# Experts ranked by rows and paired 64/64 or 96/32 in four column strips, raw rows gathered once for two passes

## The reference

```python
def grouped_moe(xn, router_w, router_bias, w1, w3, w2):      # xn = rms_norm(h, gain), 256 x 1024
    aff = sigmoid(xt @ router_w)                              # 256 x 16
    sel = aff + router_bias
    # the best group of 4 experts by the sum of its two largest sel; in it the two largest
    w = aff of the two chosen / their sum;  gate = w spread over 16 experts
    h = silu(xt @ w1[e]) * (xt @ w3[e])                       # w1, w3: 16 x 1024 x 512
    y = sum over e of (h * gate[e]) @ w2[e]                   # w2: 16 x 512 x 1024
```

## Time and profile before

| | |
|---|---|
| median of 3 runs | 566.75 us |
| the profiled execution | 565.24 us |
| its span (first to last instruction) | 563.5 us |
| mean granted TensorE clock | 0.973 |
| PE busy | 531.6 us (94%) |
| PE weight loads | 349.5 us (62%) |
| DVE, ACT busy | 208.5 us (37%), 172.6 us (31%) |
| moved by DMA | 144.67 MB |

### The profile page before, as it was taken

The page is one execution under the profiler, slowest core; times in us unless marked ns, Lnnn a source line. Parts: engine busy times, 40 slices in busy tenths (PEclk is TensorE's granted clock), DMA queues, the critical chain, the costliest instruction groups (busy, mean ns, idle before and its releaser), DMA issues.

```text
span 563.5 us, 7211 instructions
## 1 busy us (share of the span) xinstructions
PE 531.6 (94%) x2808; PEld 349.5 (62%) x2809; DVE 208.5 (37%) x314; ACT 172.6 (31%) x259; POOL 13.8 (2%) x29
## 2 busy tenths in 40 slices
PE   4999999699899999998988999999999999999994
PEld 3898998488578888887854444544444544454442
DVE  4858675657335285555381111111111111111113
ACT  3645557656714243542311111111111111111113
POOL 7100000000000000000000000000000000000000
PEclk9999999989959999999969999999999999999998
DMA  9985445213310653969870997999929979999971
GB/s 314 347 295 183 164 169 186 98 54 135 117 47 2 233 214 109 381 224 374 305 287 12 379 387 289 389 387 386 387 70 380 387 281 391 387 387 386 387 284 75
DMA packets 70950, 144.67 MB, mean 257 GB/s; under 512 B 1873, under 2 KB 3937, under 8 KB 70930
## 3 DMA queue, kind: packets, MB, share of 16 engines
q1 hardware_dynamic: 70274, 142.62, 69.9%
q0 software_dynamic: 656, 1.78, 0.9%
HBM read 143.35 MB, written 1.05 MB: 256 GB/s over the span
## 4 chain that ended last, share of the span: by engine, by line
PE 88%; DVE 5%; ACT 4%; issue 1%; DMA 1%; DVEq 0%; SPq 0%; ACTq 0%
PE bank L1448 34%; PE bank L1207 25%; PE bank L1194 9%; PE bank L1435 7%; PE bank L1511 3%; DVE ring_lo L752 1%; PE bank L1331 1%; PE bank L1330 1%; PE bank L1492 1%; DMA work<-in_norm_mix_gain 1%; PE bank L1165 1%; PE bank L1410 1%; PE bank L1475 1%; ACT diff L607 1%; PE bank L1305 1%
## 5 line engine op out<-in xcount | busy, mean ns | idle before, releaser
L1448 PE MATMUL bank<-ring,work 128*64 128x512 f32 x864 | 191.4, 595 | 2.3 <-issue 2.0
L1448 PEld LDWEIGHTS bank<-ring,work 128*64 128x64 f32 x864 | 61.7, 137 | 113.0 <-issue 111.8
L752 DVE TENSOR_TENSOR ring_lo<-ring,w_hi 128x2048 fp32r<-128x2048 f32 x38 | 86.2, 2286 | 25.7 <-ACT w_hi L550 25.7
L550 ACT ACTIVATE w_hi<-ring 128x2048 fp32r<-128x2048 f32 x37 | 70.3, 1910 | 69.2 <-PE bank L1207 42.5
L1435 PEld LDWEIGHTS bank<-work,xn 128*128 128x128 f32 x320 | 40.4, 199 | 9.2 <-issue 7.3
L1435 PE MATMUL bank<-work,xn 128*128 128x128 f32 x320 | 42.9, 286 | 0.0
L1142 DVE TENSOR_TENSOR ye_lo<-bank,ye_hi 128x512 fp32r<-128x512 f32 x18 | 12.4, 692 | 77.5 <-ACT ye_hi L717 77.5
L1207 PE MATMUL bank<-w_hi,x_hi 128*128 128x512 f32 x144 | 39.3, 395 | 0.4 <-DVE work L788 0.4
L1207 PE MATMUL bank<-w_hi,x_lo 128*128 128x512 f32 x144 | 38.6, 390 | 0.0
L1207 PE MATMUL bank<-ring_lo,x_hi 128*128 128x512 f32 x144 | 38.6, 390 | 0.0
L707 ACT ACTIVATE work<-bank 128x512 f32<-128x512 f32 x9 | 5.4, 597 | 93.9 <-PE bank L1448 93.9
(11 more groups left out here) (241 smaller groups left out, 535.1 us busy)
## 6 DMA issues: line engine op xcount, KB each, us to landing
ring<-in_moe_w SPq DMA_DIRECT2D x64, 1024.0 KB, 13.9
ring<-in_moe_w SPq DMA_DIRECT2D x16, 2048.0 KB, 15.8
ring<-in_w_in SPq DMA_DIRECT2D x13, 2048.0 KB, 8.3
ring<-in_w_out SPq DMA_DIRECT2D x2, 2048.0 KB, 11.3
ring<-in_w_in SPq DMA_DIRECT2D x2, 1024.0 KB, 6.7
ring<-in_w_up_b SPq DMA_DIRECT2D x1, 2048.0 KB, 7.5
ring<-in_w_up_c SPq DMA_DIRECT2D x1, 2048.0 KB, 7.5
ring<-in_w_up_a SPq DMA_DIRECT2D x1, 2048.0 KB, 7.5
```

Of the source, the lines that this page charges most:

```text
L550: act.activation(hi(q), raw(q), ACT.Copy).then_inc(w_hi_ready, 1)
L752: dve.tensor_tensor(lo(q), raw(q), hi(q).bitcast(F32), ALU.subtract).then_inc(w_lo_ready, 1)
L1448: last = pe.matmul(bank[e * J:(e + 1) * J, dst, :], lhsT[:, k, e * J:(e + 1) * J], rhs[e][:, k, :], start=(k == 0), stop=(k == tiles - 1))
```

## The change

*Ranking and pairing.* Experts 0 to 3 are done first, with 64 rows each, which needs no plan. The other twelve are ranked by their number of rows. The three largest get 96 rows each and are paired with the three smallest at 32, the six in between 64 each, in pairs. A *round* is two passes: x with a 64/64 pair, y with a 96/32 pair (64/64 in the first round). Four rounds do all 16 experts; what overflows goes to extra rounds. `plan` now holds the experts of each round by number.

*Strips.* The stationary operand of all expert matmuls is 32 columns wide, four strips (column tiles) a k tile, each with its owner's weights:

```diff
+    STRIPS = ((0, 0, 1, 1), (0, 0, 0, 1))
-            def two_experts(dst, lhsT, rhs, tiles, second_half=()):
-                    for e in range(2):
-                        last = pe.matmul(bank[e * J:(e + 1) * J, dst, :], lhsT[:, k, e * J:(e + 1) * J],
-                                         rhs[e][:, k, :], start=(k == 0), stop=(k == tiles - 1))
+            def strips(dst, lhsT, first, owners, rhs, k, n):
+                for j, e in enumerate(owners):
+                    cols = slice(j * STRIP, (j + 1) * STRIP)
+                    ins = pe.matmul(bank[cols, dst, :], lhsT[:, k, first + j * STRIP:first + (j + 1) * STRIP],
+                                    rhs[e][:, k, :], start=(k == 0), stop=(k == n - 1))
```

*Gather.* `xn` is gone. ACT and DVE split h into `h_hi` and `h_lo` (float32r; L945's region and after it), and the gather of a round takes both passes' 256 rows at once:

```diff
+                        for part in (h_hi, h_lo):
+                            ins = pe.matmul(bank[:, b, (k - k0) * ROWS:(k - k0 + 1) * ROWS],
+                                            part[:, a, k * P:(k + 1) * P], sel[:, a, :],
```

*Selection on DVE.* The turned selection `selT` is no longer transposed on TensorE. A ones matrix times a diagonal spreads each token's two slot numbers and its weights over all partitions once (`slot_rows`, `col_rows`, two 128x512 products in the first pass); each pass DVE compares and adds:

```diff
+                dve.tensor_scalar(same, slot_rows, col(SLOT0), None, ALU.is_equal).then_inc(rows_step, 1)
+                dve.tensor_tensor(selT[:, y, :], same[:, 0:T], same[:, T:2 * T], ALU.add).then_inc(selT_ready, 1)
+                dve.tensor_tensor(weighed, same.unsqueeze(1).to_broadcast([P, 2, 2 * T]), col_rows, ALU.mult)
+                dve.tensor_reduce(col(COLS + 2 * y, 2), weighed, AX.X, ALU.add).then_inc(cols_ready, 1)
```

*Weights.* Channel 8p + k is on partition p (4p + k for w2), so the 16 KB of a partition are contiguous, and each matrix is loaded in two parts of k tiles for both experts:

```diff
+            def load(slots, matrix, idx, landed):
+                for b in range(2):
+                    part = slice(b * 2048, (b + 1) * 2048)
+                    for e in range(2):
+                        sp.dma_start(ring[:, slots[e], part],
+                                     matrix[0, idx[e]].rearrange("(p k) n -> p (k n)", p=P)[:, part])
...
+            with sp.Fori(0, last) as m:
+                sp.wait_ge(w1_done, 2 * m + 1)
+                load(W1_SLOTS[0], moe_w1, next_x, w1_in[0])
+                sp.wait_ge(w3_done, 2 * m + 1)
+                load(W3_SLOTS, moe_w3, this_y, w3_in)
+                sp.wait_ge(y_done, 4 * m + 2)
+                load(W2_SLOTS, moe_w2, this_y, w2_in)
+                sp.wait_ge(w1_done, 2 * m + 2)
+                load(W1_SLOTS[1], moe_w1, next_y, w1_in[1])
...
```

More of the change, by code:

```diff
@@ L425, in next_w1 @@
[L425 to L438, removed]
@@ L440, in _ @@
-            sp.wait_ge(planned, 1)
[L441 to L451, removed]
@@ L455, in _ @@
+            this_y = experts((YA, YB), last)
+            sp.wait_ge(w3_done, 2 * last + 1)
+            load(W3_SLOTS, moe_w3, this_y, w3_in)
+            sp.wait_ge(y_done, 4 * last + 2)
+            load(W2_SLOTS, moe_w2, this_y, w2_in)
             for a in range(TT):
@@ L722, in _ @@
+            act.wait_ge(ld_small, 16 * 8)
+            for i, b in enumerate((6, 7, 4, 5)):
+                gathered_rows(b, 2 * i, i + 1)
+            for y in range(2):
+                expert_pass(0, y, True)
+            total = rounds(act)
+            with act.Fori(1, total) as m:
+                for y in range(2):
+                    expert_pass(m, y)
+            high_y(4 * total, 1, z_banks(1)[0])
             act.preload_act_table_set("sqrt_and_others")
@@ L1149, in _ @@
+            for y in range(2):
+                expert_pass(0, y, True)
+            total = rounds(dve)
+            with dve.Fori(1, total) as m:
+                for y in range(2):
+                    expert_pass(m, y)
+            low_y(4 * total, 1, z_banks(1)[0])
             for a in range(TT):
@@ L1429, in _, with gather @@
             sums_start(range(3, 4))
[L1431 to L1433 removed]
+            def gather(b, k0):
+                for k in range(k0, k0 + 2):
                     for a in range(TT):
[L1435 to L1439 removed]
@@ L1500, in expert_pass @@
-                for b in range(2):
-                    if b:
-                        landed(W2_SLOTS, pair * 16 + 16)
-                    two_experts(7 - b, heT, [w[:, :, b * 512:(b + 1) * 512] for w in w2], KF).then_inc(y_done, 1)
-                for b in range(2):
-                    for ready, y in ((ye_a, ye_hi), (ye_d, ye_lo)):
-                        if b and y is ye_lo:
-                            gather(1, range(4))
-                        pe.wait_ge(ready, 2 * n + 2 + b)
-                        for a in range(TT):
-                            pe.matmul(bank[:, 2 * b + a, :], selT[:, a * P:(a + 1) * P],
-                                      y[:, b * 512:(b + 1) * 512], start=False, stop=False,
-                                      skip_group_check=True)
@@ L1519, in _ @@
+            for y in range(2):
+                expert_pass(0, y, True)
+            total = rounds(pe)
+            with pe.Fori(1, total) as m:
+                for y in range(2):
+                    expert_pass(m, y)
+            scatter(4 * total, 1, 1)
             pe.matmul(bank[:, 4, 0:P], ident[:, :], ident[:, :], start=True, stop=True).then_inc(finished, 1)
```

653 lines of the change are left out of this document (410 added, 243 removed).

## The result

| | before | after |
|---|---|---|
| run, median (range), n | 566.76 us (565.04 to 569.10), 4 | 532.98 us (531.16 to 534.27), 4 |
| ratio | | 0.9405, 95% interval 0.9376 to 0.9434 |
| profiled execution: span, run | 563.5, 565.24 | 531.4, 533.18 |
| TensorE's mean clock in the span | 0.973 | 0.965 |

The forecast was 532, with a span of 529.8. I read the views in the same order as before the change.

What follows compares the result with a forecast made beforehand. TensorE bound the kernel before, DMA close behind; after, weights bind from the sixth pass. Span = 307.9 + 75.5 MB / 415 GB/s (181.9) + 40.0 = 529.8, plus 1.7 = 531.5, said as 532 us; range 521 to 550.

Steps and rivals of the forecast that it cites:

- two at a time: Rival, each k tile: strips go only two side by side, 21.1 us more a pass, 687 us in all; chance 0.04.
- the issue bound: Rival, strip instructions: 116 to 134 ns a pair, pass 27.0 to 30.4 us, total 533 to 557 us; chance 0.10.
- The extra round: Rival, passes: one expert over its cap adds a round, 25.2 MB, 61 us, total 593 us; chance 0.02.
- The slow pitch: Rival, weight loads: DMA below 350 GB/s by the 16 KiB pitch; at 250 GB/s the total is 651 us; chance 0.03.
- DMA's start: After the first w1: data flows again at 307.9 us, 1.9 us after that w1 is done at 306.0.
- The rate: Weight loads with 8 KB pieces: 415 GB/s, bounds 360 and 426, so 75.5 MB take 181.9 us.
- The rest: From w2's second half of the seventh pass to the end: 3.5, 1.0, 24.7 and 10.8, together 40.0 us.
- The pass: TensorE, one pass of two experts: 21.1 + 2.1 + 2.1 + 0.5 = 25.8 us, against 28.26 before.
- the cover of `he`: Between w3 and the transposes: `he` on DVE, 0.75 us, stays covered by half a gather, 1.05 us.
- Getting to w1: From the start through mixer, choosing and first gather: w1 starts at 298.9 us instead of 300.38.
- When TensorE meets DMA: Late passes: TensorE, 25.8 us a pass against 30.3 for DMA, first waits in the sixth, by 2 to 3 us.
- The walk of the queue: Load queue, 10.1 us per 4.19 MB: slots are free in time, so DMA goes through without idle time.

Runs made afterwards that it cites:

- the two-tile kernel: The kernel after with two column tiles of 64 in place of four strips of 32 in all expert products; 531.43 us, ratio 0.9385.
- The kernel in small pieces: The kernel after with its weight loads in 2 KB pieces for w1 and w3, 4 KB for w2; 544.44 us, ratio 0.9618.
- the first of the order kernels: The kernel after with w1 of the next y pass loaded behind w3 and w2 of the next x pass, from the second round on; 530.12 us.
- order kernels: Variants of the kernel after that change only the order of the weight loads in the queue; 530.12, 526.77 and 529.56 us.
- the staged order: The kernel after with w1 of the next y pass last in round 1, loads in TensorE's order of need from round 2; 526.77 us, ratio 0.9295.

## Why the prediction was right, and by how much each step was off

**Passes, strips, rates as bounds.** Eight passes and 7.0 us a block were as forecast; two at a time (687) and the issue bound (533 to 557) are refuted by 112 ns an instruction and by the two-tile kernel. The extra round didn't come. The slow pitch didn't either: at a pitch of 16 KiB the runs show 422 GB/s. What the Trainium skill (DMA: Bandwidth & Descriptors, "Latency and other measured facts") has for far larger pitches does not show at this one.

**The formula** was span = 307.9 + 75.5 MB / rate + 40.0 = 529.8. Its terms as measured:

- *DMA's start*: bytes flow as if from 309.4 at 422 GB/s (0.69 MB came between 308.5 and 311), +1.5 us. Of it 1.2 is w1 of the first pass, at 300.06 instead of 298.9 (see below: a slow start of 2.0 us that is not of the change).
- *The rate*: 422 instead of 415, 178.9 us instead of 181.9, −3.0. The kernel in small pieces, at 394, should by this be 12.7 us slower; it is 11 to 12. So the formula prices the rate rightly.
- *From the last byte to TensorE*: I had nothing for it. 309.4 + 178.9 = 488.3, and w2's second half of the seventh pass started at 490.8, 2.5 us later. TensorE took it without a wait, for it had waited at w3's second half, 480.71, just before: both are ties within half a microsecond, and I had named w2. The same sum with 11, 13.5, 16.5 and 17 loads of 4.19 MB puts the bytes at 418.7, 443.6, 473.4 and 478.4, 2.3 to 2.4 us ahead of each of the four landings at which TensorE waited. So some 2.35 of the 2.5 us lie between bytes and engine, and the rest is TensorE.
- *The rest*: 40.6 instead of 40.0; the longer scatters and `he` of the pass below.

309.4 + 178.9 + 2.5 + 40.6 = 531.4. The sum was 1.6 us short because errors of 1.5, 2.5 and 0.6 met one of −3.0. That the total came so near is thus in part luck: the term that I had at nothing and the rate that I took too low nearly cancel. Without the slow start the terms as measured would give an estimated 529.4, 0.4 under the forecast. Its form is what the runs confirm: a different rate moves the end as the formula says, and a shorter pass (0.27 us) doesn't move it by an amount that can be told.

**The pass** is 26.25 us, not 25.8. The blocks are as forecast (21.05). The two scatter halves are 1.14 each, not 1.05 (+0.2). The step that failed is the cover of `he`: from w3's end to the transposes 1.31 us pass (+0.26), because DVE needs 1.13, and TensorE's half gather, 1.05, is over before it. I had taken 0.75 from the same operation of the kernel before and did not see that the new one writes with a stride. The transposes are 0.66, not 0.5; the second half gather 0.95. I had written that DVE ending a wait inside a pass would show this wrong, and it does: 1.14 in each pass's chain. Its total load was right: 5.7 and 8.6 us of two passes.

**Getting to w1.** The first gather took 4.22 instead of 5.23, the clock being back at 0.97 from 296.5 on, and w1 followed at once, as forecast. But everything in the mixer was 2.6 us later by then. 2.0 of it arises in the first projection (25.32 us for its 192 instructions, 23.32 before). The stretch from 15 to 20 us, after and before:

```profile
15.00:20.00 5.00, 4.45 (x21) 4.45 (x22) 5.00 (x5) 3.69 (x4) 4.75 (x5) 1.00 1.06 312
```

```profile
15.00:20.00 5.00, 4.49 (x37) 4.49 (x38) 4.99 (x5) 3.65 (x3) 1.22 (x3) 1.00 1.10 286
```

In the same busy time 21 instructions run instead of 37. It isn't the change: the same stretch has 40 instructions in the kernel after with pieces and 22 in the kernel before with contiguous weights. It comes and goes from one profiled execution to the next with the same code around it; why is open. The profile of the kernel before, from which the forecast was made, has the quick start, and that of the kernel after the slow one. The other 0.6 I didn't trace. The splitting of h, with its output reordered again, took ACT 1.11 us and DVE 1.07 a piece where I had 0.6 and 0.69; the last two pieces stand in the chain with 1.10 and 1.06 us, about where xn's 2.47 us went, so little of it reached w1.

**When TensorE meets DMA.** Forecast: first in the sixth pass, by 2 to 3 us. Measured: first in the fifth, 1.3 us, then 2.0 in the sixth and 1.8 and 1.3 in the seventh, plus 1.8 for the clock that fell after the second. Neither stalls nor clock before 480.7 cost the end anything, as I had written of a pass that waits for weights anyway; in the first of the order kernels, where no later landing ties the end, the same clock cost its full 1.8.

**The walk of the queue** held: no hole in DMA from 311 to 507 us. But I only asked when slots are free, not whether the order is the one in which TensorE needs them. The order kernels show that 5.7 us lay there (532.52 to 526.77, on one chip). In the staged order the last bytes come between 509 and 510 (74 GB/s in that microsecond, 0 in the next), and the last w2's second half starts at 510.7, behind them by less than the 2.5 us above. So there, by this reading, the bytes themselves end the kernel, and another order has nothing left to win; that was not tried.

## What to carry to other kernels

- Two limits that lie close together must be moved together. Price each edit by itself and both together: here one gave 0.8 us, the other 16.4, both 29.1, and a third edit worth 14 us of TensorE gave 4.8.
- When an edit changes the layout of a load, work out the run in memory for each matrix by itself: the same line gave 2 KB for two of them and 4 KB for the third.
- When transfers bind the end, write the end as "first byte + bytes up to the tie / rate + what follows", and then ask of each load in the queue who waits for it first. Put the load that is needed last behind the others, but only from where the engine has caught up with DMA; before that an order that waits for a slot makes a hole.
- An operation's price goes with its access pattern and not only with its shape: look at the step of its output before taking a duration over.

## What the runs showed of the hardware that I had not expected

- One core sustained 422 GB/s over 150 us with 8 KB runs in HBM, against 386 to 387 with 2 KB pieces and 409 with 4 KB pieces of w2, all at full DMA share (1.01, 1.05 and 1.02).
- At four landings the engine that waited started 2.3 to 2.4 us behind where the bytes end by their rate.
- Four 128x32 f32 tiles run side by side: 112 ns an instruction of 512 columns; a weight load of 32 columns shows 110 ns.
- A write in steps of 512 bytes costs DVE 1126 ns instead of 751 for 128x512 in f32. TensorE's transposes read f32 with a step of 16 bytes at no cost.
- A stall of 1.96 us in the middle of full load was followed by 4 us at a granted clock of 0.60, one of 3.68 us by 0.52 and 0.63; stalls of 1.3 and 1.8 us by no change. The length of the stall does not decide it alone: in the kernel with small pieces a stall of 3.37 us left the clock at 1.00 and the half block at 3.64, and one of 3.35 us brought 0.55 and 9.06 us for a block of 7.0:

```profile
453.45 3.64 PE L1611 MATMUL bank<-ring,work 128*32 128x512 f32 x32 [3.37 <-DMA ring<-in_moe_w]
...
485.38 9.06 PE L1611 MATMUL bank<-ring,work 128*32 128x512 f32 x64 [3.35 <-DMA ring<-in_moe_w]
```

- At the start of the program 21 or 37 instructions of the same kind run in 5 us while the granted clock of the stretch reads 1.00 both times, a difference of 2 us in the span.
